# Attention scores from three products of rounded halves instead of one plain f32 product

## What is computed

```python
# first block (the sparse attention; its selection covers all 8 blocks of 64 keys here)
ss  = einsum('qghd,gqkd->gqhk', q, k_sel) * 64 ** -0.5
p_s = softmax(where(k_pos <= t, ss, NEG))        # 8 query heads, 2 groups of keys
sw  = einsum('qghd,kgd->gqhk', q, k_win) * 64 ** -0.5
p_w = softmax(where(wmask, sw, NEG))
o   = g0 * o_c + g1 * (p_s @ v_sel) + g2 * (p_w @ v_win)
# second block, second layer (forgetting attention, 16 heads, each with keys of its own)
logits = einsum('bhqd,bhkd->bhqk', q, k) + (c_q - c_k)
p = softmax(where(causal, logits, -inf))
o = p @ v
```

## Time and profile before

| what | value |
|---|---|
| median of 3 runs | 2058.88 us (2057.05 to 2061.43) |
| the profiled execution's own time | 2057.08 us |
| its span | 2055.2 us |
| TensorE busy | 2026.5 us (99%) |
| VectorE busy | 1181.4 us (57%) |
| ScalarE busy | 796.5 us (39%) |
| GpSimd busy | 27.0 us (1%) |

### The profile page before, as it was taken

How to read it: one execution, slowest core, us unless ns; L and a number is a source line. 1 busy time by engine, 2 the same in 40 slices (tenths; PEclk the granted TensorE clock), 3 DMA queues, 4 the chain that set the end, 5 groups by cost and what they waited for, 6 DMA issues and landing times.

```text
span 2055.2 us, 25553 instructions
## 1 busy us (share of the span) xinstructions
PE 2026.5 (99%) x9922; PEld 1647.7 (80%) x9922; DVE 1181.4 (57%) x1801; ACT 796.5 (39%) x1297; POOL 27.0 (1%) x58
## 2 busy tenths in 40 slices
PE   9999999999999999999999999999999999999998
PEld 8865878888888888877888888878886588888886
DVE  6777645454445356556565764764525857476475
ACT  4258242332212223245542432443324844243343
POOL 1000000000000000000000000000000000000000
PEclk9999999999999999999999999999999999999999
DMA  7310412322222222321323222231322132322222
GB/s 252 108 42 20 140 36 103 113 91 95 101 103 82 102 103 73 122 87 58 113 73 113 85 100 102 97 118 52 114 103 92 42 113 73 112 102 83 101 102 72
DMA packets 39425, 194.87 MB, mean 95 GB/s; under 512 B 4744, under 2 KB 13096, under 8 KB 19840
## 3 DMA queue, kind: packets, MB, share of 16 engines
q1 hardware_dynamic: 36240, 183.34, 25.3%
q0 software_dynamic: 2880, 9.88, 1.7%
q10 hardware_dynamic: 208, 0.33, 0.1%
HBM read 188.83 MB, written 2.15 MB: 93 GB/s over the span
## 4 chain that ended last, share of the span: by engine, by line
PE 93%; DVE 3%; ACT 2%; DVEq 1%; DMA 1%; issue 1%; SPq 0%; ACTq 0%
PE bank L443 26%; PE bank L444 26%; PE bank L445 26%; PE bank L1514 2%; PE bank L1501 2%; PE bank L1482 1%; PE bank L529 1%; PE bank L530 1%; PE bank L534 1%; DVE w_lo L391 1%; PE bank L2509 1%; ACT w_hi L372 1%; PE bank L2501 1%; PE bank L1707 0%; ACT work L1581 0%
## 5 line engine op out<-in xcount | busy, mean ns | idle before, releaser
L372 ACT ACTIVATE w_hi<-w_raw 128x2048 fp32r<-128x2048 f32 (+3 forms) x165 | 302.2, 1832 | 721.6 <-PE bank L445 679.0
L443 PE MATMUL bank<-a_hi,w_hi 128*128 128x512 f32 (+1 forms) x1408 | 540.6, 384 | 0.0
L445 PE MATMUL bank<-a_hi,w_lo 128*128 128x512 f32 (+1 forms) x1408 | 537.8, 382 | 0.0
L444 PE MATMUL bank<-a_lo,w_hi 128*128 128x512 f32 (+1 forms) x1408 | 537.8, 382 | 0.0
L391 DVE TENSOR_TENSOR w_lo<-w_raw,w_hi 128x2048 fp32r<-128x2048 f32 (+3 forms) x163 | 358.6, 2201 | 254.7 <-ACT w_hi L372 254.7
L445 PEld LDWEIGHTS bank<-a_hi,w_lo 128*128 128x128 f32 x1408 | 264.7, 188 | 51.7
L443 PEld LDWEIGHTS bank<-a_hi,w_hi 128*128 128x128 f32 x1408 | 264.8, 188 | 51.3 <-issue 0.8
L444 PEld LDWEIGHTS bank<-a_lo,w_hi 128*128 128x128 f32 x1408 | 264.8, 188 | 50.0
L443 PE MATMUL bank<-w_hi,big_halves 128*128 128x512 f32 x384 | 150.2, 391 | 0.3 <-DVE w_lo L391 0.3
L445 PE MATMUL bank<-w_hi,big_halves 128*128 128x512 f32 x384 | 149.5, 389 | 0.0
L444 PE MATMUL bank<-w_lo,big_halves 128*128 128x512 f32 x384 | 149.4, 389 | 0.0
(11 more groups left out here) (384 smaller groups left out, 2556.9 us busy)
## 6 DMA issues: line engine op xcount, KB each, us to landing
w_raw<-in_w_fu SPq DMA_DIRECT2D x44, 1024.0 KB, 4.8
w_raw<-in_w_up SPq DMA_DIRECT2D x16, 1024.0 KB, 4.8
w_raw<-in_w_down SPq DMA_DIRECT2D x16, 1024.0 KB, 4.8
w_raw<-in_w_fd SPq DMA_DIRECT2D x16, 1024.0 KB, 4.8
w_raw<-in_w_fd SPq DMA_DIRECT2D x8, 768.0 KB, 4.2
w_raw<-in_w_rqk SPq DMA_DIRECT2D x4, 1024.0 KB, 5.3
w_raw<-in_w_rvg SPq DMA_DIRECT2D x4, 1024.0 KB, 5.0
w_raw<-in_w_gate SPq DMA_DIRECT2D x4, 1024.0 KB, 4.8
```

The lines of the kernel that those rows point to most:

```text
L372: act.activation(dst[0][:, cols], raw[slot][:, cols], ACT.Copy).then_inc(hi_half_ready.sem if half == 0 else hi_ready.sem, 1)
L443: pe.matmul(out, w[0], x[0], start=first, stop=False)
L444: pe.matmul(out, w[0], x[1], start=False, stop=False)
L445: return pe.matmul(out, w[1], x[0], start=False, stop=last)
```

## The change

Each score becomes three float32r matmuls: high half of q by high half of k, high by low, low by high, summed in PSUM. The matmuls of the two heads still alternate, each on its 64 rows. The halves have to be made first ("staged"): a high half is a copy that rounds to float32r, a low half is the plain value less the high half.

- For pair 0, ACT makes the high halves and DVE the low ones, in the late functions of block 2 of the dense stage before (`begin_act`, `begin_dve`). In nsa the two tiles of keys serve all pairs (`static`); they are made here once for all.
- For pairs 1 to 7, POOL makes both: in nsa a copy and a subtraction (the queries alone), in fox two of each (queries and keys), all of 128 x 512. POOL starts on pair 1 when the last block of the dense stage is evacuated, on pair n when the scores of pair n - 2 are done; the tiles alternate between odd and even pairs.
- In fox POOL issues the bias DMAs of pair n after it has staged pair n.
- PE's score of a pair's first unit waits for `staged`.

```diff
-                    if u == 0:
-                        pe.wait_ge(*ready)
+                    if u % G == 0:
+                        pe.wait_ge(staged.sem, b_st + staged_for(n))
                     if u >= 2:
                         pe.wait_ge(max_ready.sem, b_m + 2 * (u - 1))
-                    for i, w, at in members(u):
-                        for e in range(2):
-                            last = pe.matmul(out[e][:, at:at + w], q[heads[e], i * P:(i + 1) * P], k[heads[e], 0:w],
-                                             start=at == 0, stop=not causal and (i, at) == GROUPS[u % G][-1])
+                    for a, b in ((0, 0), (0, 1), (1, 0)):
+                        for i, w, at in members(u):
+                            for e in range(2):
+                                last = pe.matmul(out[e][:, at:at + w], q[a][heads[e], i * P:(i + 1) * P], k[b][heads[e], 0:w],
+                                                 start=a == 0 and b == 0 and at == 0,
+                                                 stop=not causal and a == 1 and (i, at) == GROUPS[u % G][-1])
...
+            def stage_low(dve, n):
+                for r, (st, src) in enumerate(stagings(n)):
+                    dve.wait_ge(high_staged.sem, b_hi + once + n * each + r + 1)
+                    dve.tensor_tensor(st[1], src, st[0].bitcast(F32), ALU.subtract).then_inc(staged.sem, 1)
+
+            def begin_dve(dve):
+                if static:
+                    for p in range(2):
+                        k = held[p][1]
+                        dve.wait_ge(high_staged.sem, b_hi + p + 1)
+                        dve.tensor_tensor(k[1], k_of(p), k[0].bitcast(F32), ALU.subtract).then_inc(staged.sem, 1)
+                stage_low(dve, 0)
...
+            def gpsimd(pool):
+                for n in range(1, pairs):
+                    if n == 1:
+                        pool.wait_ge(evacuated.sem, b_e)
+                    else:
+                        pool.wait_ge(scores_ready.sem, b_s + G * (n - 1))
+                    for st, src in stagings(n):
+                        pool.tensor_copy(st[0], src).then_inc(high_staged.sem, 1)
+                    for r, (st, src) in enumerate(stagings(n)):
+                        pool.wait_ge(high_staged.sem, b_hi + once + n * each + r + 1)
+                        pool.tensor_tensor(st[1], src, st[0].bitcast(F32), ALU.subtract).then_inc(staged.sem, 1)
+                    if bias_next is not None:
+                        bias_next(pool, n)
+
+            def stage_high(act, n):
+                for st, src in stagings(n):
+                    act.activation(st[0], src, ACT.Copy).then_inc(high_staged.sem, 1)
+
             def begin_act(act):
+                if static:
+                    for p in range(2):
+                        act.activation(held[p][1][0], k_of(p), ACT.Copy).then_inc(high_staged.sem, 1)
+                stage_high(act, 0)
+
                 act.activation(warm[:, :], one[:, :], ACT.Exp)
...
@@ nsa
+            space = [big_tiles(1, 4 * r, 4, F32R) for r in range(2)]
+                             lambda n: [[x[:, r + n % 2, :] for x in space] for r in (0, 2)], factor, finish, True,
...
@@ fox
+                def space(n):
+                    if n == 0:
+                        return [[fx_first[:, r + h, :] for h in range(2)] for r in (0, 2)]
+                    return [[x[:, r + n % 2, :] for x in (a_hi, a_lo)] for r in (0, 2)]
...
-                def next_bias_rows(pool):
-                    for n in range(1, FH // 2):
-                        if n < 3:
-                            pool.wait_ge(evacuated.sem, b_evac + 4)
-                        else:
-                            pool.wait_ge(max_ready.sem, b_max + 2 * 3 * (n - 1))
-                        bias_rows(pool, n)
+                def next_bias_rows(pool, n):
+                    if n >= 3:
+                        pool.wait_ge(max_ready.sem, b_max + 2 * 3 * (n - 1))
+                    bias_rows(pool, n)
...
-                stages.append(dense("fq", two_chunks(a_tiles), scaled_by(qT, float(FD) ** -0.5), none, none, begins(begin_high)))
-                stages += [attend, {"gpsimd": next_bias_rows}, {"scalar": split_high, "vector": lambda dve: split_low(dve, [KT - 1])}]
+                stages.append(dense("fq", two_chunks(a_tiles), scaled_by(qT, float(FD) ** -0.5), begins(begin_dve), none, begins(begin_high)))
+                stages += [attend, {"scalar": split_high, "vector": lambda dve: split_low(dve, [KT - 1])}]
```

More of the change, by code:

```diff
@@ L237, in build @@
         with ExitStack() as same:
+            sb(same, "shared_probs", [P, 4352])
+            fx_first = sb(same, "fx_first", [P, 4, S], F32R)
+        with ExitStack() as same:
             sb(same, "shared_front", [P, 4096])
@@ L271, in build @@
         gains_in, weights_in = tally("gains_in"), tally("weights_in")
[L272 removed]
+        positions_in, high_staged, den_ready = (tally(n) for n in ("positions_in", "high_staged", "den_ready"))
         scaled, updated, split_hi_done, split_lo_done = (tally(n) for n in ("scaled", "updated", "split_hi_done", "split_lo_done"))
@@ L275, in build @@
         keys_staged = tally("keys_staged")
-        scores_ready, max_ready, probs_ready = (tally(n) for n in ("scores_ready", "max_ready", "probs_ready"))
+        staged, scores_ready, max_ready, probs_ready = (tally(n) for n in ("staged", "scores_ready", "max_ready", "probs_ready"))
         probs_turned, probs_copied, out_ready, out_done = (tally(n) for n in ("probs_turned", "probs_copied", "out_ready", "out_done"))
@@ L1427, in rotate, with attention @@
             return dve.tensor_tensor(x, x, swapped_x, ALU.add)
-        def attention(turns_n, q_of, k_of, v_of, ready, factor, finish, together, lent, probs, free, bias_of, bias_ready=None, causal=False, ends=None):
+        def attention(turns_n, q_of, k_of, v_of, static, space, factor, finish, together, lent, probs, free, bias_of, bias_ready=None, bias_next=None, causal=False, ends=None):
             GROUPS = (((0, 0), (1, P)), ((2, 0),), ((3, 0),))
@@ L1443, in attention @@
             score_bank, turn_bank, out_bank = bank[0:4], bank[4:6], (bank[7], bank[6])
-            b_s, b_m, b_p = scores_ready.n, max_ready.n, probs_ready.n
+            b_st, b_s, b_m, b_p, b_hi = staged.n, scores_ready.n, max_ready.n, probs_ready.n, high_staged.n
             b_n, b_t, b_c, b_o, b_d = weighted.n, probs_turned.n, probs_copied.n, out_ready.n, out_done.n
@@ L1447, in attention, with staged_for, stagings @@
             heads = [slice(64 * e, 64 * e + 64) for e in range(2)]
+            held = [space(n) for n in range(pairs)]
+            once = 2 if static else 0
+            each = 1 if static else 2
+            def staged_for(n):
+                return once + each * (n + 1)
+            def stagings(n):
+                q, k = held[n]
+                return [(q, q_of(n))] + ([] if static else [(k, k_of(n))])
             def members(u):
@@ L1603, in scalar @@
                 steps(LAG + 1, step)
+            staged.n += staged_for(pairs - 1)
+            high_staged.n += staged_for(pairs - 1)
             scores_ready.n += groups
@@ L1610, in attention @@
             out_done.n += turns_n if together else pairs
-            return {"tensor": tensor, "vector": vector, "scalar": scalar}, begin_act
+            return {"tensor": tensor, "vector": vector, "scalar": scalar, "gpsimd": gpsimd}, begin_act, begin_dve
         def region(off, *shape):
@@ L1916, in first_projections, with nsa @@
             return stages + [attention_stage]
-        def nsa(o, vg, gate, ready, free):
+        def nsa(o, vg, gate, free):
             qk = big_tiles(0)
+            space = [big_tiles(1, 4 * r, 4, F32R) for r in range(2)]
             def factor(n, e, i):
@@ L3039, in build @@
         sigs = [work4[:, 0:2, :], work4[:, 2:4, :], region(5120, 2, S), region(5120 + 2 * S, 2, S)]
-        stages = first_projections(o, vg, gate, tables, lambda ready, free: nsa(o, vg, gate, ready, free))
+        stages = first_projections(o, vg, gate, tables, lambda free: nsa(o, vg, gate, free))
         more, *begin = retention(o, tables, sigs)
```

18 lines of the change are left out of this document (9 added, 9 removed).

## The result

The changed kernel takes 2077.16 us (median of five runs, 2075.92 to 2078.17) against 2058.88 before (five runs too, 2057.05 to 2061.43): ratio 1.0089, 95% interval [1.0078, 1.0101]. It is slower by 0.9%, 13 us above the upper end of the range. The profiled execution took 2078.17 us, its span is 2076.3 us. In the changed kernel the scores are at L1497, the mask at L1503, the transposes at L1517, the values at L1530, the maximum at L1566, the scalings at L1579 (second attention) and L1581 (first), and GpSimd's copies and subtractions at L1609 and L1612.

The account below looks back on a forecast made before the run. TensorE was taken as the bound, only just so in the first attention. +2.0 (start) - 1.5 (second attention) - 0.6 (first) = -0.1 us gave 2058.8 us against the 2058.88 median, range 2054.0 to 2064.0.

Parts of the forecast that it names:

- Scores after: TensorE's scores as three float32r products: 0.73, 0.89 and 0.90 us, together 0.24 us less a pair.
- rival 2: Float32r matmuls on 64 rows don't run the two heads side by side: +22.5 us, 2081; chance 8%.
- rival 4: Float32r matmuls of 128 columns run at a quarter of the pace: +2.5 us, 2061.3; chance 7%.
- Second attention, start: Pair 1 waits for GpSimd's four staging instructions (3.6 us) and the bias DMAs behind them: 2.0 us lost.
- Pair 0's staging and GpSimd's wake: Before the attentions: pair 0's staging costs nothing, done while ScalarE and VectorE idle; GpSimd's first elementwise instruction isn't late.
- Rival 5: GpSimd's first elementwise instruction starts about 6 us late, delaying the first attention's pair 1: +5 us, 2063.8; chance 5%.
- Rival 1: The gain is kept in both attentions, with 128-column matmuls at 0.067 us and a free start: -4.8 us, 2054.1; chance 20%.
- Second attention, steady part: Pairs 2 to 7, bounded by TensorE, gain 0.24 us each: 1.5 us gained.
- First attention, steady part: Six pairs gain 0.1 of the 0.24 us each, with ScalarE close behind and VectorE slowed by GpSimd: 0.6 us gained.
- Rival 3: VectorE's scalings wait for GpSimd's instructions in both attentions, losing more than VectorE's slack: +5.9 us, 2064.8; chance 18%.

Follow-up runs that it names:

- new scores alone: Changed kernel, but GpSimd stages only pair 1 in each attention and pairs 2 to 7 read its halves again; 2057.4 us, ratio 0.9999.
- copies alone: Changed kernel with each of GpSimd's subtractions replaced by a second copy of the same tile; 2065.29 us, ratio 1.0040.
- both shape variants: Changed kernel with each scaling one column less (2075.93 us), or reading three gapped rows of an odd number of columns (2065.24 us); one run each.
- the one with pair 1 unstaged: Changed kernel, staging from pair 2 held until a chosen unit is weighed, early bias DMAs, second attention's pair 1 scored in plain f32; 2055.37 us, ratio 0.9987.
- the one with early subtractions: Changed kernel with VectorE subtracting the low halves of pairs 1 to 7, one unit earlier than in a 2083.97 us version; GpSimd only copies; 2061.38 us.

## Why the prediction was wrong

- **Scores after**: right. 0.73, 0.90, 0.89 us; the gain is 0.26 us a pair in the second attention (0.24 forecast) and 0.5 us over the first (0.6). The heads run side by side, so rival 2 is out, and so is rival 4. For the first unit the sum is right by luck: where 0.11 us was taken for a matmul of 128 columns and 0.12 for one of 256, the next one starts 0.06 us after the first kind in two of three products and 0.17 after the second (new scores alone, at 1598.7 us).
- **Second attention, start**: right in the new scores alone, 1.9 us for 2.0. GpSimd takes 3.7 us for the four (3.6), and both waits are where they were put, 1.3 us of TensorE (1.4) and 1.4 of VectorE (2.2). In the changed kernel the first distance is 9.27 us, 3.1 over the kernel before: TensorE waits the same 1.3 us, but then runs at half clock (1583.8 to 1594.1 us), and GpSimd, which stages pair 2 at once, holds the scalings of pair 0 for 2.3 us more. Issuing the bias rows first doesn't mend it, since the staging, which is then later, holds the first weighing; only without the staging of pair 1 does the first distance come back to 6.15 us.
- **Pair 0's staging and GpSimd's wake**: nothing is lost there; with the new scores alone the first attention's first distance is 6.39 us as before, and the profiled span is that of the kernel before, the very sum of the prediction. Rival 5 is out. Rival 1 is too: it needed a start that costs nothing.
- **Second attention, steady part**: this step failed. "From pair 3 on GpSimd has 3.6 + 1.1 us of work in a period of 7.8" counts GpSimd's work as if it cost only GpSimd. Its copies and subtractions hold VectorE's scalings: +2.07 us a pair against the new scores alone (9.84 to 7.77).
- **First attention, steady part**: the same, with a term far too small. "VectorE, which loses something to GpSimd; I take 0.1 us of the 0.24" allowed 0.14 us a pair for the loss; it was 1.05 us a pair of held scalings and up to 0.85 of period (8.42 against 7.57 with the new scores alone).
- **Rival 3 had the mechanism, and the wrong price.** It forecast 0.9 and 1.8 us a pair held; in the steady part it was 1.05 and 2.6. And it took off a slack of 0.77 and 1.3 us, worked out from VectorE's busy share, and arrived at 2064.8. The slack was much smaller: in the second attention 2.62 us of hold made the period 2.07 us longer than with the new scores alone, and with copies alone 1.30 us made it 0.74 longer, so some 0.55 us was absorbed both times; in the first attention it was some 0.2 (1.04 and 0.36 of hold, 0.85 and 0.17 of period). The hold lies in the chain from score over maximum, exponential and scaling to the transposes, and TensorE, which takes the transposes three units behind the score, waits for just this scaling (1.85 us in the pair shown). A share of 84% says that VectorE is idle at some time, not that it is idle then. Where its extra work lay at another point of the order, 1.36 us a pair of it made the periods 0.0 to 0.9 us longer, 0.5 on the mean.
- **What the prediction left out besides**: the stretches at half clock. The changed kernel has 20.5 us of them inside the two attentions, the one before none; what they cost is inside the 4.8 and 12.9 us (one of the second attention's periods is 11.46 us where its neighbours are 9.84, with a stretch of 3.4 us in it). Why one comes at 95 us, in unchanged code and with TensorE busy all through, isn't settled: the changed kernel and five of its variants have it; the new scores alone, both shape variants, the one with pair 1 unstaged and the one with early subtractions don't. The 2.0 us in front of the first attention and the 1.5 us between the two go with these stretches. The kernel that scales one column less has neither of them and the same periods as the changed one, and its span is still 18.8 us over the kernel before. So most of the 21.1 us is there without them, and the periods above don't hang on them.

## What to carry to other kernels

Work given to an idle GpSimd is not free while VectorE runs SBUF-to-SBUF instructions in its fast mode: look in the order of both engines for what runs at the same moment, and put GpSimd's work beside VectorE's reads of PSUM. Slack counts only where it lies on the waiting chain: an engine at 84% had 0.55 us of a period of 8 for a delay of the instruction that the next engine waits for, where its busy share seemed to leave 1.3.

## What the hardware showed that was not expected

- A scaling of 128 columns, 0.28 us alone, can be held over several GpSimd instructions in a row: 3.09 us across one copy and two subtractions, ending with the last of them. VectorE got nothing in between them. In the changed kernel one scaling got through behind each GpSimd instruction.
- An odd number of columns does not take VectorE out of the fast mode (0.52 ns a column in both); a view of three rows of an odd length does (1.04).
- The maximum, with one operand in PSUM and one in SBUF, is not stretched at all by a subtraction beside it (mean 681 ns for 512 columns in the changed kernel, 684 in the one before; 683 in the four that lay mostly beside GpSimd's instructions).
- float32r matmuls on 64 rows run two heads side by side; three products of 512 columns for two heads take 0.90 us, of 128 and 256 columns 0.89.
